# Attention of the sample sequences with key positions on partitions, pages of keys and values in one gather

## What is computed

```python
def stick_breaking(q, k, v, q_pos, k_pos, bias):
    z = einsum('bqhd,bkhd->bhqk', q, k) * dh ** -0.5 + bias
    valid = k_pos[None, :] < q_pos[:, None]
    log_keep = where(valid, log_sigmoid(-z), 0.0)
    after = cumsum(log_keep, axis=3, reverse=True) - log_keep
    wts = where(valid, exp(log_sigmoid(z) + after), 0.0)
    return einsum('bhqk,bkhd->bqhd', wts, v)
```

## Time and profile before

| | us |
|---|---|
| median of 3 runs (3414.50 to 3427.53) | 3415.54 |
| profiled execution, its time | 3408.59 |
| its span, first to last instruction | 3406.8 |
| TensorE busy (78% of the span) | 2666.7 |
| VectorE busy (45%) | 1542.0 |
| GpSimd busy (29%) | 994.5 |
| ScalarE busy (20%) | 697.5 |
| DMA engines, mean rate | 252 GB/s |

### The profile page before, as it was taken

How to read it: one execution, slowest core, us unless ns; L and a number is a source line. 1 busy time by engine, 2 the same in 40 slices (tenths; PEclk the granted TensorE clock), 3 DMA queues, 4 the chain that set the end, 5 groups by cost and what they waited for, 6 DMA issues and landing times. The chain is left out here.

```text
span 3406.8 us, 25784 instructions
## 1 busy us (share of the span) xinstructions
PE 2666.7 (78%) x8145; PEld 1410.6 (41%) x8145; DVE 1542.0 (45%) x3743; ACT 697.5 (20%) x1550; POOL 994.5 (29%) x859
## 2 busy tenths in 40 slices
PE   7877778887867778777788958986857777877776
PEld 2353244445622333333336747864543333333333
DVE  0112222221276667767631434133146666666663
ACT  1113333321211212222111122120121211211211
POOL 0000043320044444444420033200014444444441
PEclk9988889898989888989989968558979989888998
DMA  6435354423299999999963301423249999999994
GB/s 215 147 101 197 106 180 153 157 96 99 83 412 414 404 395 396 409 407 419 412 276 93 120 21 38 111 62 99 81 176 405 413 407 402 399 390 400 414 407 176
DMA packets 219164, 859.75 MB, mean 252 GB/s; under 512 B 16484, under 2 KB 98877, under 8 KB 137102
## 3 DMA queue, kind: packets, MB, share of 16 engines
q0 software_dynamic: 102400, 721.47, 53.1%
q1 hardware_dynamic: 116673, 137.21, 12.6%
HBM read 845.50 MB, written 13.18 MB: 252 GB/s over the span
## 5 line engine op out<-in xcount | busy, mean ns | idle before, releaser
L1849 POOL DMA_INDIRECT exp_uv<-in_peer_uv_dram,expert x640 | 771.7, 1206 | 1331.9 <-PE exp_acc L1880 819.4
L1879 PE MATMUL exp_acc<-exp_uv,exp_diag 128*128 128x512 f32 x1280 | 744.9, 666 | 404.2 <-ACT exp_diag L1896 403.7
L1930 DVE CUSTOM_DVE_ANT_0 exp_uv<-exp_uv,htok 128x1024 f32<-128x1024 f32 x640 | 772.0, 1226 | 500.1 <-DMA exp_uv<-in_peer_uv_dram,expert 491.5
L1880 PE MATMUL exp_acc<-exp_uv,exp_diag 128*128 128x512 f32 x1280 | 709.2, 638 | 0.0
L1879 PEld LDWEIGHTS exp_acc<-exp_uv,exp_diag 128*128 128x128 f32 x1280 | 253.7, 209 | 795.7 <-ACT exp_diag L1896 531.2
L1880 PEld LDWEIGHTS exp_acc<-exp_uv,exp_diag 128*128 128x128 f32 x1280 | 266.4, 208 | 351.8 <-issue 351.8
L1888 ACT ACTIVATE exp_act<-exp_dots 128x4 f32<-128x4 f32 x160 | 32.9, 205 | 1180.2 <-DVE exp_dots L1930 1180.2
L1896 ACT ACTIVATE exp_diag<-ident,exp_w 128x128 f32<-128x128 f32 x640 | 201.8, 386 | 0.0
L501 PE MATMUL ssd_in_ps<-hT,ssd_in_w 128*128 128x320 f32 x640 | 174.9, 437 | 10.4 <-ACT hT L398 10.4
L501 PE MATMUL peer_q_ps<-hT,peer_q_w 128*128 128x320 f32 x512 | 142.9, 443 | 20.8 <-ACT hT L398 20.8
L501 PEld LDWEIGHTS ssd_in_ps<-hT,ssd_in_w 128*128 128x128 f32 x640 | 122.9, 192 | 62.5 <-issue 12.7
(11 more groups left out here) (402 smaller groups left out, 2646.7 us busy)
## 6 DMA issues: line engine op xcount, KB each, us to landing
ada_w<-in_ada_w_dram SPq DMA_DIRECT2D x12, 2048.0 KB, 7.9
attp_w<-in_ada_w_dram SPq DMA_DIRECT2D x12, 2048.0 KB, 7.8
ssd_in_w<-in_ssd_w_in_dram SPq DMA_DIRECT2D x20, 1024.0 KB, 5.3
peer_q_w<-in_peer_wq_dram SPq DMA_DIRECT2D x16, 1024.0 KB, 5.4
ab_in_w<-in_ab_w_in_dram SPq DMA_DIRECT2D x10, 1024.0 KB, 5.1
exp_uv<-in_peer_uv_dram,expert POOLq DMA_INDIRECT x640, 9.2
out_ssm_sample_dram<-state_hd SPq DMA_DIRECT2D x8, 1024.0 KB, 5.2
ssd_out_w<-in_ssd_w_out_dram SPq DMA_DIRECT2D x4, 2048.0 KB, 8.3
```

Source lines behind the costliest of these rows:

```text
L1849: pool.indirect_dma_start(slot(g)[:], None, table, bass.IndirectOffsetOnAxis(ap=experts[:, g:g + 1], axis=0)).then_inc(landing(g)[0], 16)
L1879: pe.matmul(acc[t % 2][0][:], diag[g % (2 * GRP)][:], slot(g)[:, D:D + 512], start=False, stop=False, skip_group_check=True)
L1880: pe.matmul(acc[t % 2][1][:], diag[g % (2 * GRP)][:], slot(g)[:, D + 512:2 * D], start=False, stop=False, skip_group_check=True).then_inc( ...
L1930: dve.tensor_tensor_reduce(slot(g)[:, 0:D], slot(g)[:, 0:D], m.htok[:, t, :], 1.0, 0.0, ALU.mult, ALU.add, dots[:, i % 2, k:k + 1]).then_i ...
```

## The change

Keys and values of one page come in one gather of 128 rows of 6 KB, 8 per sequence in place of 16, into `kv`, which has room for the pages of two sequences; a page is freed for the sequence after next as soon as it is mixed. The host stores each page of keys turned: row p holds, for each of the 6 chunks of 128 dimensions, dimension p of the 128 positions. So a page of keys is the stationary operand as it lands, and the 16 moving columns are the queries of the chunk's two heads (8 each). The scores come out with the positions on the partitions and 96 rows along the free dimension, nine blocks (8 pages and the new keys). No transposes are left. The sum from the end is a matmul with a triangle of ones (`onward`) over the block itself, and one with all ones over `later`, the running sum of the blocks behind, which VectorE makes with eight additions. For mixing, the values of a page are the stationary operand (128x128 per chunk), the weights the 16 moving columns, accumulated over pages in one bank. The queries of all eight sequences are laid out once, in `operands`. All loops are written out for eight sequences; in each turn TensorE mixes sequence b - 1, sums the suffix of b, and scores b + 1. The new values are loaded onto 64 partitions.

```diff
@@ -200,19 +198,13 @@
...
-                link(pool.memset(m.headmask[:], 1.0))
...
-                link(pool.memset(hsel[:], 1.0))
...
+                link(pool.affine_select(out=m.onward[:], in_=m.ones[:], compare_op=ALU.is_ge, fill=0.0,
+                                        base=0, pattern=[[-1, P]], channel_multiplier=1))
+                link(pool.memset(m.far_t[:], 0.0))
+                link(pool.affine_select(out=m.far_t[:], in_=m.far_t[:], compare_op=ALU.is_gt, fill=FAR,
+                                        base=0, pattern=[[SQ, NSEQ], [1, SQ]], channel_multiplier=-1))
+                link(pool.affine_select(out=m.far_t[:], in_=m.far_t[:], compare_op=ALU.is_ge, fill=FAR,
+                                        base=0, pattern=[[-SQ, NSEQ], [0, SQ]], channel_multiplier=1))
@@ -809,263 +795,246 @@
+class AttendSample:
...
+    COLS = HB * SQ
...
+        self.far = s.sb("far", [TS, NSEQ, cols])
+        self.kv = s.sb("kv", [P, 2 * PAGES, 2 * D_B])
+        self.vnew = s.sb("vnew", [TS, D_B])
+        self.qb = s.sb("qb", [P, NSEQ, CH * 2 * SQ])
+        self.z = [s.sb(f"z{i}", [P, 9 * cols]) for i in range(2)]
+        self.w = [s.sb(f"wT{i}", [P, 9 * cols]) for i in range(2)]
...
+        self.cuts = ((0, 5 * cols), (5 * cols, 9 * cols))
+    def loads(self, sp):
...
+        sp.dma_start(self.vnew[:], a["v_sample"].rearrange("n b t h d -> (n b t) (h d)")).then_inc(self.loaded, 16)
+
+    def page(self, b, j):
+        return (b % 2) * PAGES + j
+
+    def fetch(self, pool, b):
+        table = self.a["cache_kv"].rearrange("g p x -> (g p) x")
+        for j in range(PAGES):
+            if b >= 2:
+                pool.wait_ge(self.pagedone, PAGES * (b - 2) + j + 1)
+            pool.indirect_dma_start(self.kv[:, self.page(b, j), :], None, table,
+                                    bass.IndirectOffsetOnAxis(ap=self.rows[:, b * PAGES + j:b * PAGES + j + 1], axis=0)).then_inc(self.landed[self.page(b, j)], 16)
+
+    def score(self, pe, b):
+
+        W = 2 * SQ
+        if b == 0:
+            pe.wait_ge(self.opset, 4)
+        for j in range(PAGES):
+            pe.wait_ge(self.landed[self.page(b, j)], 16 * (b // 2 + 1))
+            if b and j in (0, 5):
+                pe.wait_ge(self.zset, 3 * (b - 1) + (1 if j == 0 else 3))
+            half, jj = (0, j) if j < 5 else (1, j - 5)
+            for c in range(self.CH):
+                o = jj * self.COLS + c * W
+                ins = pe.matmul(self.psz[half][:, o:o + W], self.kv[:, self.page(b, j), c * P:(c + 1) * P], self.qb[:, b, c * W:(c + 1) * W], start=True, stop=True)
+            ins.then_inc(self.kread, 1)
+        for c in range(self.CH):
+            o = 3 * self.COLS + c * W
+            ins = pe.matmul(self.psz[1][0:TS, o:o + W], self.m.proj[:, 8 + c, TP:T], self.qb[:, b, c * W:(c + 1) * W], start=True, stop=True)
+        ins.then_inc(self.scored, 1)
+
+    def suffix(self, pe, b):
+
+        pe.wait_ge(self.tailed, 9 * b + 9)
+        for half, (lo, hi) in enumerate(self.cuts):
+            if b:
+                pe.wait_ge(self.expo, 2 * (b - 1) + half + 1)
+            pe.matmul(self.psu[half][:, 0:hi - lo], self.m.onward[:], self.sp_[:, lo:hi], start=True, stop=False)
+            pe.matmul(self.psu[half][:, 0:hi - lo], self.m.ones[:], self.later[:, lo:hi], start=False, stop=True).then_inc(self.summed, 1)
+
+    def mix(self, pe, b):
+
+        W = 2 * SQ
+        w, o = self.w[b % 2], self.pso[b % 2]
+        pe.wait_ge(self.weighed, b + 1)
+        if b >= 2:
+            pe.wait_ge(self.done, 2 * (b - 1))
+        for j in range(PAGES):
+            for c in range(self.CH):
+                ins = pe.matmul(o[:, c * W:(c + 1) * W], self.kv[:, self.page(b, j), D_B + c * P:D_B + (c + 1) * P],
+                                w[:, j * self.COLS + c * W:j * self.COLS + (c + 1) * W], start=(j == 0 and c == 0), stop=False, skip_group_check=True)
+            ins.then_inc(self.pagedone, 1)
+        for c in range(self.CH):
+            ins = pe.matmul(o[:, c * W:(c + 1) * W], self.vnew[:, c * P:(c + 1) * P],
+                            w[0:TS, PAGES * self.COLS + c * W:PAGES * self.COLS + (c + 1) * W], start=False, stop=True, skip_group_check=True)
+        ins.then_inc(self.mixed, 1)
+
+    def soften(self, act, b):
+        act.wait_ge(self.zset, 3 * b + 3)
+        if b:
+            act.wait_ge(self.softp, b)
+        act.activation(self.e[:], self.z[b % 2][:], ACT.Abs).then_inc(self.actd, 1)
+        act.wait_ge(self.actd, 2 * b + 1)
+        act.activation(self.e[:], self.e[:], ACT.Exp, scale=-1.0).then_inc(self.actd, 1)
+        act.wait_ge(self.actd, 2 * b + 2)
+        act.activation(self.e[:], self.e[:], ACT.Ln, bias=1.0).then_inc(self.logged, 1)
+
+    def weigh(self, act, b):
+        act.wait_ge(self.expo, 2 * b + 2)
+        if b >= 2:
+            act.wait_ge(self.mixed, b - 1)
+        act.activation(self.w[b % 2][:], self.z[b % 2][:], ACT.Exp).then_inc(self.weighed, 1)
+
...
+    def logits(self, dve, b):
+        z, cols, scale = self.z[b % 2], self.COLS, HD ** -0.5
+        if b >= 2:
+            dve.wait_ge(self.weighed, b - 1)
+        dve.wait_ge(self.kread, PAGES * b + 5)
+        dve.scalar_tensor_tensor(out=z[:, 0:5 * cols].rearrange("p (g x) -> p g x", x=cols),
+                                 in0=self.psz[0][:, 0:5 * cols].rearrange("p (g x) -> p g x", x=cols), scalar=scale,
+                                 in1=self.bias[:].unsqueeze(1).broadcast_to([P, 5, cols]), op0=ALU.mult, op1=ALU.add).then_inc(self.zset, 1)
+        dve.wait_ge(self.scored, b + 1)
+        dve.scalar_tensor_tensor(out=z[:, 5 * cols:8 * cols].rearrange("p (g x) -> p g x", x=cols),
+                                 in0=self.psz[1][:, 0:3 * cols].rearrange("p (g x) -> p g x", x=cols), scalar=scale,
+                                 in1=self.bias[:].unsqueeze(1).broadcast_to([P, 3, cols]), op0=ALU.mult, op1=ALU.add).then_inc(self.zset, 1)
+        dve.scalar_tensor_tensor(out=z[0:TS, 8 * cols:], in0=self.psz[1][0:TS, 3 * cols:4 * cols], scalar=scale,
+                                 in1=self.far[:, b, :], op0=ALU.mult, op1=ALU.add).then_inc(self.zset, 1)
+
+    def softplus(self, dve, b):
+        z, cols = self.z[b % 2], self.COLS
+        dve.wait_ge(self.zset, 3 * b + 3)
+        dve.wait_ge(self.logged, b + 1)
+        if b:
+            dve.wait_ge(self.summed, 2 * b)
+        dve.scalar_tensor_tensor(out=self.sp_[:], in0=z[:], scalar=0.0, in1=self.e[:], op0=ALU.max, op1=ALU.add).then_inc(self.softp, 1)
+        dve.wait_ge(self.softp, b + 1)
+        for g in range(7, -1, -1):
+            dve.tensor_tensor(self.later[:, g * cols:(g + 1) * cols], self.later[:, (g + 1) * cols:(g + 2) * cols],
+                              self.sp_[:, (g + 1) * cols:(g + 2) * cols], ALU.add).then_inc(self.tailed, 1)
+            dve.wait_ge(self.tailed, 9 * b + 8 - g)
+        dve.nop().then_inc(self.tailed, 1)
+
+    def exponent(self, dve, b):
+        z = self.z[b % 2]
+        for half, (lo, hi) in enumerate(self.cuts):
+            dve.wait_ge(self.summed, 2 * b + half + 1)
+            dve.tensor_tensor(z[:, lo:hi], z[:, lo:hi], self.psu[half][:, 0:hi - lo], ALU.subtract).then_inc(self.expo, 1)
+
+    def outputs(self, dve, b):
+        dve.wait_ge(self.mixed, b + 1)
+        for h in range(2):
+            r = slice(64 * h, 64 * h + 64)
+            dve.tensor_copy(self.m.yT[r, 2:8, TP + b * SQ:TP + (b + 1) * SQ],
+                            self.pso[b % 2][r, 0:self.COLS].rearrange("p (c x) -> p c x", x=2 * SQ)[:, :, SQ * h:SQ * h + SQ]).then_inc(self.done, 1)
+
 def stage_attend_sample(nc, m, a):
...
-        kp = s.sb("kp", [P, PAGES, D_B])
-        vp = s.sb("vp", [P, PAGES, D_B])
...
+                t.find_rows(pool)
+                for b in range(NSEQ):
+                    t.fetch(pool, b)
...
+                t.score(pe, 0)
+                for b in range(NSEQ):
+                    if b:
+                        t.mix(pe, b - 1)
+                    t.suffix(pe, b)
+                    if b + 1 < NSEQ:
+                        t.score(pe, b + 1)
+                t.mix(pe, NSEQ - 1)
...
+                t.soften(act, 0)
+                for b in range(NSEQ):
+                    t.weigh(act, b)
+                    if b + 1 < NSEQ:
+                        t.soften(act, b + 1)
...
+                t.operands(dve)
+                t.logits(dve, 0)
+                t.softplus(dve, 0)
+                for b in range(NSEQ):
+                    if b:
+                        t.outputs(dve, b - 1)
+                    t.exponent(dve, b)
+                    if b + 1 < NSEQ:
+                        t.logits(dve, b + 1)
+                        t.softplus(dve, b + 1)
+                t.outputs(dve, NSEQ - 1)
...
@@ -2130,6 +2098,10 @@
     arrays, aps = {}, {}
     inputs = dict(inputs)
     inputs["peer_uv"] = np.concatenate([np.asarray(inputs["peer_u"]), np.asarray(inputs["peer_v"])], axis=-1)
+    k = np.asarray(inputs["cache_sb_k"])
```

(54 more changed lines are left out.)

257 lines of the change are left out of this document (63 added, 194 removed).

## The result

| | before | after |
|---|---|---|
| median of 7 runs, us | 3415.54 | 3455.43 |
| lowest to highest | 3409.17 to 3427.53 | 3439.89 to 3466.08 |
| profiled execution, us | 3408.59 | 3453.54 |
| its span | 3406.8 | 3451.7 |
| sample attention ends at (last output copy) | 767.1 | 808.0 |

The change makes the kernel 1.1% slower: the ratio of the runs is 1.0109, 95% interval 1.0081 to 1.0136. The forecast was 3467 (3430 to 3500), slower with a chance of 0.82. In the two traces the stage ends 41 us later, and the whole execution took 45 us longer; the last 4 are a drift of the later stages: what follows the stage takes between 2637 and 2657 us in the traces here.

What follows compares the result with a forecast made beforehand. Sample attention was taken as bound by TensorE's own instruction stream. Its terms summed to an end at 846, less 27 for full-clock stretches: 819 against 767.1, 52 us later; 3460 profiled, 3467 as median (3430 to 3500).

Steps and rivals of the forecast that it cites:

- Price of a record at 1.2 GHz: Scores and mixing: each trace record (weight load with matmul) takes 0.216 us, half for 128x64 weights; 16 moving columns hide beside it.
- The clock: Sample attention on TensorE: narrow matmuls run at 1.2 GHz, as at line 1502; mean granted clock 0.52 to 0.60.
- first rival: Sample attention: clock stays at 2.4 GHz, 27.7 us a sequence, stage ends near 663, 3312 in all; chance 0.11.
- Start: Sample attention: TensorE starts at 425.5 us, with 2 us off for loading new values and 1 on for the larger page.
- Exposed chain: Before the first suffix: logits, softplus and block additions keep TensorE waiting once, 8.8 us.
- End wait: End of sample attention: mixing waits once for exponent and weights, 2.5 us.
- Gathers: Page loads in sample attention: 16 us a sequence against 47 of TensorE, nothing exposed after the first page.
- Cycle: One sequence of sample attention on TensorE: 51.1 us at 1.2 GHz against 41.2 before; near 47 expected in the trace.
- Returns of the clock: After each sequence's dense suffix: 3.4 us at 2.4 GHz, eight times, taking 27 us off the stage.
- second rival: Suffix gives back 6.8 us at full clock a sequence, or narrow matmuls partly hold it: 3441; chance 0.13.
- main case: Sample attention mostly at 1.2 GHz, 3.4 us at full clock per sequence: stage ends at 819, 3467 in all; chance 0.50.
- The sum without returns: Sample attention: start, scores, waits, suffixes and mixing, all at 1.2 GHz, put the stage's end at 846 us.

## Why the prediction was right

The rows named the bound and the price, and both held; one term of the sum was too small. By its steps:

- *Price of a record at 1.2 GHz*, 0.216 us: 0.215 measured, and 0.108 for 64 columns of weights (0.11). 16 columns cost nothing. At 2.4 GHz it is 0.113 with 96 columns (0.118). One premise was weaker than it read: the 128 columns of line 1511 would by the rate of the earlier trace rows take 0.21 us by themselves, so its 6.90 us could not show that 64 contraction rows save nothing. The runs do: the 12 records with 64x128 weights and 16 columns take 2.67 us (548.61 to 551.28), 0.22 each.
- *The clock*, taken from line 1502 and not from the row of the old stage: 0.50 in the blocks, 0.55 in the stage (0.52 to 0.60). The first rival, which had TensorE's unbroken work keep 2.4 GHz, fell for the change; its price was sound: it put the end of the stage at 663 and the cycle at 27.7, and with 96 columns they are 664 and 27.3.
- *Start* 425.5: 424.74, and 422.9 in the second trace of the same kernel, so the match is no better than that. *Exposed chain* 8.8: the wait was 8.4. *End wait* 2.5: 1.6. *Gathers* never late: so, but for 0.2 us. *Cycle* with a return of 3.4 us, 51.1 - 3.4 = 47.7: 47.8.
- *Returns of the clock*, 3.4 us each, 27 in all: this term was too small. Four of the eight were twice as long, 41 us. The second rival had this mechanism with 54 us, and the truth lies halfway between it and the main case.

The sum without returns, 846, can be checked. With the suffix cut there was no return, and the stage ended at 805; with the 39 us of suffix put back that is 844 (an estimate). From there the 41 us at the full clock took 36 off, down to 808. That is nearly one for one, as a cycle shows: without a return it would be 46.1 + 4.9 = 51.0 us, with a short one it was 47.8, with a long one 44.7. So the forecast of 819 was late by 11 us: 2 for the half-clock work, 9 for the returns. The change with split gathers had the eight short returns of the forecast, and its stage ended at 821.7 and 820.9.

End of stage plus time at full clock is 849 for the change, 847 for its second trace, 849 and 848 with split gathers, 849 with 32 columns; with the suffix twice 894, which is 848 + 46; with half the load 758, which is 849 - 91; with 48 columns it is 854, 5 more, of which 2 are the slower cycle and 1 a later start. So in all of them the stage costs a nearly fixed amount of half-clock work, and what differs is mostly how long the full clock came back.

In the whole time the forecast was 12 us above the median. The stage gives 11 of them, the drift of the later stages 4 the other way, and the median lay 2 us above the profiled execution and not 7, which gives the other 5. The time alone would not have chosen between the main case (3467) and the second rival (3441): 3455 lies in the middle. The trace does, and it says half of each.

What the large change bought is thus plain. It took away 384 transposes, their copies and the wide matmuls, and halved the work of VectorE, ScalarE and GpSimd in the stage; at the full clock the stage ends 103 us before the old one, as the version with 96 columns does (664.0 against 767.1). The change gave all of this back, and 41 us more, through the clock. The missing piece was to keep the moving operand wide.

## What to carry to other kernels

Before a rewrite that makes data the stationary operand, count weight loads times weight columns, and look in the trace for a stretch of the kernel that already runs with so few moving columns and no wide matmuls in between: its granted clock is the one to cost with, not the clock of the stage that is being replaced. Where the load hides the stream, wider moving operands are nearly free (here up to 96 columns beside 128 columns of weights), even when the added columns are zeros or are never read, and they can be worth more than the rewrite itself. If a cost seems to sit in one piece, take it out and watch the clock: here removing most of a dense piece that looked like 46 us was worth 3.

## What the runs showed of the hardware that was not expected

- Beside the same loads of 128x128 weights the stage had a mean granted clock of 0.57 with 48 moving columns and of 0.97 with 96; widths between were not tried.
- Around a dense suffix the full clock came back for either 3.4 or 6.8 us. The change had four of each in both of its traces, in another order; with the gathers split all eight were short in both traces, without a wait of TensorE for a gather; with the suffix twice as long all were 6.8 us and none longer.
- Zeros among the moving columns did not lower the clock: with 96 columns in the scores, of which 80 are zeros, a block of scores ran at 1.00, and the mixing with 16 columns behind it fell to 0.53.
